# A fixed third expert, and routing tables in other buffers, in a two-layer diffusion backbone with a mixture of experts

## The chip, the cores and the metric

The kernel runs on one core of a Trainium2 chip. The metric is the device time of one execution in microseconds; the number given for a kernel is the median of its runs. Lower is better.

## The reference, cut to what matters

Two layers work on 512 tokens of width 1024 (and 256 context tokens in the first), all in float32. Each layer has a mixer (layer 0: attention beside a convolution; layer 1: a short gated convolution) and then a mixture of 16 experts, of which every token uses two:

```python
def moe_ffn(h, router_w, router_bias, w_gate, w_up, w_down):
    e_idx, e_w = route(h, router_w, router_bias)      # top 2 of 16 experts for each of 512 tokens
    ...                                               # rows sorted by expert, padded to whole blocks
    def expert_block(args):
        tok, e = args
        xb = jnp.take(h, tok, axis=0, mode="fill", fill_value=0)
        return (jax.nn.silu(xb @ w_gate[e]) * (xb @ w_up[e])) @ w_down[e]
    ...
    y = out[dest].reshape(n_tok, TOP_K, -1) * e_w[..., None]
    return y.sum(axis=1)
```

`w_gate[e]` and `w_up[e]` are 1024 x 512, `w_down[e]` is 512 x 1024: three pieces of 2 MB for each expert. Which expert a token uses is known only when the layer's mixer and its norm are done. The order in which the experts are worked through is free.

## The kernel before, in words

**Blocks.** The kernel pads each expert's rows to blocks of 64 (the reference has 256). Experts with no token get one block, so that every expert is loaded and passed once. Experts are worked through in an order of 16 *positions*. Positions 0 and 1 are always experts 0 and 1. The other fourteen are ranked by their number of blocks and taken alternately from the two ends of the ranking: the smallest, the largest, the second smallest, and so on (constants `rank_tie` and `rank_at`, lines 93 to 97; the ranking itself on VectorE in `route`, lines 1078 to 1119).

**Weight buffers.** There are three sets of three 2 MB buffers, and position p uses set p modulo 3. Two sets are slots of `ring`. The third, used by positions 2, 5, 8, 11 and 14, is `mid` (gate weights), `hT_cat` (up weights) and `big` (down weights). These three buffers have other uses before: `hT_cat` holds the transposed tokens until the router's product ("route", l, 0), `big` holds the normalised tokens until they have been stored to `xhat_d` in DRAM, and `mid` holds tables of the routing.

**The loading queue.** SyncE issues all weight loads, in program order, from `load_experts` (line 481). For each layer: positions 0 and 1 as soon as the ring slots come free during the mixer and the first products of the routing; then a wait for `route_ready` (all tables made) and for two gathers of tokens (`hg_in` at 32), a read of the third expert's number from `order_i`, and the three loads of position 2 (lines 498 to 504). From position 3 on, `load_next` waits for each piece until the same piece of three positions ago has been used (`used[k]`: gate, up and down products counted), and `two_before` lets no more than two loads be in flight.

**Routing.** TensorE makes the router's logits, VectorE goes through about a hundred small dependent steps (line 1018 on), TensorE counts and spreads the tables, and the last step signals `route_ready`. The tables are seven: `oh_slot`, `in_blk`, `oh_blk`, `val_blk`, `ranks_above`, `oh_order`, `order_tmp`. All seven are views of `mid`. Smaller vectors are views of `apad` (`rtmp`).

**The expert loop.** GpSimd gathers 64 rows of a block (as 128 half rows, 256 KB) from `xhat_d` by an indirect DMA into `kv_buf` (line 1277), ScalarE copies them on (line 751), TensorE transposes them (line 1589), VectorE and ScalarE scale them into `hgT` (lines 1139 and 742), and TensorE makes the gate product (line 1604), the transposes of the block before (line 1611), the up product (1604 again) and the down product of the block before (line 1620). So an expert's down product comes one block after its gate and up products. VectorE scales the result and GpSimd scatters it to `y_d` (line 1287). `kv_buf` and `prob` hold the keys, values and probabilities of the attention in layer 0 and are idle during routing, except that half of `prob` holds the router's rows until line 1562 has read them.

Of the kernel before, what the change touches and what calls it, by code (L numbers as in the profile page):

```python
# [26 lines left out]
P = 128  # L27
# [6 lines left out]
KT = TT + CT  # L34
# [5 lines left out]
APAD = SEQ + 2 * PAD  # L40
SC_K = 3
NE, NG, EPG = 16, 4, 4
BLK = 64
MAXB = SEQ * 2 // BLK + NE
NB = MAXB + 3
# [19 lines left out]
def build_consts():  # L65

    p = np.arange(P)
    parts = []

    def add(name, a):  # L70
        a = np.asarray(a, np.float32).reshape(P, -1)
        at = sum(x.shape[1] for x in parts)
        CONSTS[name] = (at, at + a.shape[1])
        parts.append(a)

    add("ident", np.eye(P))
    add("ones", np.ones((P, P)))
    add("before", p[:, None] < p[None, :])

    add("sel_both", np.stack([p % 32 == 0, p % 32 == 1], 1))  # L80
    add("sel_x", np.repeat((p % 32 == 0)[:, None], P, 1))
    add("sel_expert", p[:, None] % 32 == np.arange(NE)[None, :])
    add("slot_of_col", np.tile(p % BLK, (P, 1)))

    add("half", p // BLK)
    add("out_offset", p // BLK + 2 * NIDX)
    add("full_blocks", np.tile(np.arange(SEQ // BLK) * BLK - (np.arange(SEQ // BLK) == 0), (P, 1)))
    add("block_slots", np.tile(np.arange(NB + 1) * BLK, (P, 1)))
    add("group_key", np.tile(NG - np.arange(NG), (P, 1)))
    add("expert_key", np.tile(NE - np.arange(NE), (P, 1)))  # L90


    rank_at = [0, 1] + [r for k in range((NE - 2) // 2) for r in (NE - 1 - k, 2 + k)]
    add("rank_at", np.tile(rank_at, (P, 1)))
    tie = NE - 1 - np.arange(NE)
    tie[0:2] = NE * (MAXB + 1) * np.array([3, 2])
    add("rank_tie", np.tile(tie, (P, 1)))
    add("expert_id", np.tile(np.arange(NE), (P, 1)))
    add("expert_before", np.tile((np.arange(NE)[None, :] < np.arange(NE + 1)[:, None]).ravel(), (P, 1)))
    token = np.arange(TT)[None, :, None] * P + p[:, None, None] + np.zeros((1, 1, 2))  # L100
    token = token.transpose(0, 2, 1)
    add("token_row", 2 * token)
    add("out_row", 2 * (token + SEQ * np.arange(2)[None, :, None] - NIDX))
    add("minus_half", np.full((P, 1), -0.5))
    t = np.arange(SEQ)
    inv = (np.float32(10000.0) ** (-np.arange(HD // 4, dtype=np.float32) / np.float32(HD // 4))).astype(np.float32)
    ang = np.concatenate([(t // GRID_W).astype(np.float32)[:, None] * inv,
                          (t % GRID_W).astype(np.float32)[:, None] * inv], -1).astype(np.float32)
    for name, f in (("cos", np.cos), ("sin", np.sin)):
        add(name, f(ang.astype(np.float64)).reshape(TT, P, HD // 2).transpose(1, 0, 2))  # L110
    return np.ascontiguousarray(np.concatenate(parts, 1))
# [62 lines left out]
GROUP_AT = {name: n for n, name in enumerate(GROUPS)}  # L174
# [3 lines left out]
def hybrid_backbone_kernel(nc, x, c, ctx, c_ctx, w_mod, b_mod, norm_mix_g, norm_ffn_g, ev_w_in,  # L178
# [4 lines left out]
    with stack:  # L183
# [11 lines left out]
        mid = sb("mid", [P, 4096])  # L195
# [88 lines left out]
        start_cmp = rtmp(NE + 1, NE)  # L284
        start_f = rtmp(NE + 1)
        place2, blk2, slot2, w2 = (rtmp(2, TT) for _ in range(4))
        assert rt_at[0] <= 4 * APAD

        mid_at = [0]

        def mtmp(**shape):

            n = int(np.prod(list(shape.values())))
            a = mid[:, mid_at[0]:mid_at[0] + n]
            mid_at[0] += n
            return a.rearrange(f"p ({' '.join(shape)}) -> p {' '.join(shape)}", **shape)

        oh_slot = mtmp(n=8, s=P)
        in_blk = mtmp(n=8, b=NB + 1)
        oh_blk = mtmp(n=8, b=NB)  # L300
        val_blk = mtmp(n=8, v=3, b=NB)
        ranks_above = mtmp(e=NE, o=NE)
        oh_order = mtmp(j=NE, e=NE)
        order_tmp = mtmp(j=NE, e=NE)
        assert mid_at[0] <= 4096

        def const(name):
            a, b = CONSTS[name]
# [155 lines left out]
        def _(sp):  # L464
# [16 lines left out]
            def load_experts(l, next_units):  # L481
                def two_before(i, par, k):


                    if k < 2:
                        par, k = par - 1, k + 1
                    else:
                        k = 0
                    slot = EXPERT_SETS[l][par % 3][k]
                    sp.wait_ge(unit_in[slot], i * 16 + (moe_base[l][slot] + (1 if par >= 0 else 0)) * 16)  # L490

                for par in range(2):
                    for k, w in enumerate(("wg", "wu", "wd")):
                        prev = unit_prev[(w, l, par)]
                        sp.wait_ge(acc_done, GROUP_AT[unit_last[prev]] + 1)
                        load_third(l, par, par, k)

                sp.wait_ge(route_ready[l], 1)
                sp.wait_ge(xhat_stored[l], 16 * TT)
                sp.wait_ge(hg_in[l], 32)  # L500
                e = sp.value_load(order_i[0:1, 2:3], min_val=2, max_val=NE - 1)
                for k in range(3):
                    two_before(0, 2, k)
                    load_third(l, e, 2, k)
                used = (gate_done[l], up_done[l], down_done[l])

                def load_next(j, i, par):

                    e = sp.value_load(order_i[0:1, bass.ds(j, 1)], min_val=2, max_val=NE - 1)
                    end = sp.value_load(block_start[0:1, bass.ds(j - 2, 1)], min_val=1, max_val=MAXB)  # L510
                    for k in range(3):
                        two_before(i, par, k)
                        sp.wait_ge(used[k], end)
                        load_third(l, e, par, k)

                with sp.Fori(1, NE // 3) as i:
                    for par in range(3):
                        load_next(i * 3 + par, i, par)
                load_next(NE - 1, NE // 3, 0)
                end = sp.value_load(block_start[0:1, NE - 2:NE - 1], min_val=NE - 2, max_val=MAXB)  # L520
                total = sp.value_load(block_start[0:1, NE:NE + 1], min_val=NE, max_val=MAXB)
                for k, name in enumerate(next_units[0:3]):
                    sp.wait_ge(used[k], end)
                    load_dense(name)
                sp.wait_ge(down_done[l], total)

                sp.wait_ge(y_stored[l], total * 16 + 16)
                for t in range(TT):
                    for k in range(2):
                        rows = y_d[l][(k * SEQ + t * P) * 2:(k * SEQ + (t + 1) * P) * 2, :].rearrange("(p h) n -> p (h n)", h=2)  # L530
                        sp.dma_start(y_in[t][:, k, :], rows).then_inc(yin[l][t], 16)  # L531
                for name in next_units[3:]:
                    load_dense(name)
# [1176 lines left out]
```

## Time and profile before

| | us |
|---|---|
| median of 3 runs | 1397.66 |
| lowest and highest run | 1397.36, 1401.35 |
| span of the profiled execution | 1399.6 |
| TensorE matmul busy | 1237.5 (88%) |
| TensorE weight load busy | 642.5 (46%) |
| VectorE, ScalarE, GpSimd busy | 434.6, 349.9, 334.8 |

The profiled execution has no separate time of its own beside its span of 1399.6 us, which lies 1.9 us over the median of the runs and between their lowest and highest. Matmul busy time is an upper bound of useful work, since matmuls are pipelined and their ends are modelled.

The page also cuts the span into 40 slices of 35 us; each digit is a busy share in tenths (9 is 90% or more), PEclk the granted TensorE clock in tenths of full speed, DMA the share of the 16 DMA engines. The expert stages are slices 14 to 22 and 32 to 39:

```
PE   4899969888898399999999769999985799999992
PEclk9999986887799699999999989999997899999996
DMA  9918771110014299879899680401335798989995
```

### The profile page before, as it was taken

The page shows a single profiled execution, that of the slowest core. Times are in us where ns is not written, and L with a number is a line of the kernel's source. Part 1 is how long each engine was busy: PE and PEld are TensorE (multiplying, and loading weights), DVE is VectorE, ACT ScalarE, POOL GpSimd, SP SyncE. Part 2 cuts the span into 40 slices and gives each one's busy share as a digit, 9 for nine tenths or more (in the row PEclk, how much of TensorE's full clock was granted, in tenths as well). Part 3 has the DMA queues.
Part 4 walks back from the last instruction along what each step waited for, and adds up shares of the span by engine and source line. Part 5 has one row for each costly group of instructions (what it writes and reads, how often), then busy time and mean ns, then how long its engine had stood idle before and what let it go on. Part 6 is the DMA issues. An engine that isn't in the chain of part 4 may idle for free. (4 is left out here: it accounts for less than half of the span.)

```text
span 1399.6 us, 18544 instructions
## 1 busy us (share of the span) xinstructions
PE 1237.5 (88%) x6619; PEld 642.5 (46%) x6620; DVE 434.6 (31%) x951; ACT 349.9 (25%) x670; POOL 334.8 (24%) x491
## 2 busy tenths in 40 slices
PE   4899969888898399999999769999985799999992
PEld 1744425444444255555555334444442455555550
DVE  1222775763223422222222241111226122222223
ACT  2311115564402132222222220000011322222220
POOL 1000059940000123333333220000010333333331
PEclk9999986887799699999999989999997899999996
DMA  9918771110014299879899680401335798989995
GB/s 336 352 61 297 262 282 61 61 61 0 1 60 164 105 392 389 319 289 347 319 394 395 251 333 0 163 18 57 124 105 195 272 388 324 366 324 391 396 367 194
DMA packets 138558, 322.47 MB, mean 230 GB/s; under 512 B 7452, under 2 KB 8520, under 8 KB 138514
## 3 DMA queue, kind: packets, MB, share of 16 engines
q1 hardware_dynamic: 127250, 294.44, 57.1%
q0 software_dynamic: 8640, 23.09, 4.5%
q10 hardware_dynamic: 2624, 4.33, 0.8%
q8 instruction: 30, 0.49, 0.1%
q14 instruction: 14, 0.11, 0.0%
HBM read 307.15 MB, written 19.92 MB: 234 GB/s over the span
## 5 line engine op out<-in xcount | busy, mean ns | idle before, releaser
L1604 PE MATMUL bank<-ring,apad 128*64 128x256 f32 x2176 | 251.7, 385 | 6.3 <-ACT apad L742 3.2
L1604 PEld LDWEIGHTS bank<-ring,apad 128*64 128x64 f32 x2176 | 156.3, 139 | 99.7 <-issue 29.0
L1682 PE MATMUL bank<-hT_cat,ring 128*128 128x512 f32 x384 | 165.0, 592 | 1.0 <-ACT hT_cat L612 1.0
L1620 PE MATMUL scores<-ring,apad 128*64 128x512 f32 x544 | 124.2, 598 | 1.9 <-DVE apad L1156 1.9
L742 ACT ACTIVATE apad<-scores,modcol,mod_a 128x64 f32<-128x64 f32 x208 | 67.2, 403 | 210.3 <-PE scores L1589 210.3
L1682 PEld LDWEIGHTS bank<-hT_cat,ring 128*128 128x128 f32 x384 | 72.9, 190 | 92.5 <-issue 91.4
L1274 POOL COPY cur_idx<-row_i 128x1 int32 (+1 forms) x56 | 10.1, 181 | 383.2 <-ACT apad L751 307.2
L1238 POOL TENSOR_SCALAR stats<-stats 128x1 f32<-128x1 f32 x18 | 8.5, 471 | 343.9 <-ACT mid L602 332.8
L1162 DVE SCALAR_TENSOR_TENSOR prob<-scores,slot_w,qT 128x512 f32<-128x512 f32 x50 | 37.6, 751 | 132.8 <-PE scores L1620 132.8
L925 DVE SCALAR_TENSOR_TENSOR mid<-apad,taps,mid 128x512 f32<-128x512 f32 x90 | 75.6, 880 | 0.6
L1152 DVE TENSOR_TENSOR apad<-apad,bank 128x256 f32<-128x256 f32 x50 | 21.1, 421 | 175.6 <-PE bank L1604 175.6
L1620 PEld LDWEIGHTS scores<-ring,apad 128*64 128x64 f32 x544 | 36.4, 136 | 65.6 <-issue 65.6
L1277 POOL DMA_INDIRECT kv_buf<-xhat_d,cur_idx x56 | 59.5, 1063 | 28.4 <-issue 27.2
L1156 DVE COPY apad<-bank 128x256 f32<-128x256 f32 x50 | 21.2, 425 | 144.8 <-PE bank L1611 144.8
L760 ACT ACTIVATE apad<-bank 128x256 f32<-128x256 f32 x50 | 19.2, 384 | 186.5 <-PE bank L1604 186.5
L760 ACT ACT_TABLE_LOAD x50 | 64.2, 1283 | 0.9
L1470 PE MATMUL scores<-kv_buf,qT 64*128 64x256 f32 (+1 forms) x128 | 63.4, 627 | 0.0
L1139 DVE TENSOR_SCALAR apad<-bank,mod_a,modcol 128x64 f32<-128x64 f32 x208 | 57.2, 338 | 19.1 <-PE scores L1589 14.7
L1282 POOL TENSOR_TENSOR kv_buf<-prob,cst 128x512 f32<-128x512 f32 x52 | 53.7, 1032 | 35.3 <-DVE prob L1162 35.2
L1287 POOL DMA_INDIRECT y_d<-kv_buf,cur_idx x52 | 54.9, 1055 | 28.3 <-issue 28.3
L1604 PE MATMUL bank<-hT_cat,apad 128*64 128x256 f32 x512 | 58.8, 382 | 0.0
L1620 PE MATMUL scores<-big,apad 128*64 128x512 f32 x256 | 58.5, 598 | 0.0
(248 smaller groups left out, 1557.9 us busy)
## 6 DMA issues: line engine op xcount, KB each, us to landing
ring<-in_w_mod SPq DMA_DIRECT2D x24, 2048.0 KB, 17.3
ring<-in_moe_w_gate SPq DMA_DIRECT2D x22, 2048.0 KB, 11.6
ring<-in_moe_w_up SPq DMA_DIRECT2D x22, 2048.0 KB, 11.8
ring<-in_moe_w_down SPq DMA_DIRECT2D x22, 2048.0 KB, 11.2
mid<-in_moe_w_gate SPq DMA_DIRECT2D x10, 2048.0 KB, 11.3
hT_cat<-in_moe_w_up SPq DMA_DIRECT2D x10, 2048.0 KB, 12.0
big<-in_moe_w_down SPq DMA_DIRECT2D x10, 2048.0 KB, 11.4
ring<-in_od_w_in SPq DMA_DIRECT2D x6, 2048.0 KB, 19.2
```

The source lines that it names most:

```text
L742: act.activation(hgT[:, j, :], hg_act_ps[:, at:at + BLK], ACT.Identity, bias=shift_of(l, 3, 0)(j), scale=mod_a[:, 1 + 2 * l, j:j + 1]).the ...
L760: act.activation(silu_g, gate_ps[:, 0:256], ACT.Silu).then_inc(silu_ready[l], 1)
L925: ins = V.scalar_tensor_tensor(out=conv_y[:, i, :], in0=src, scalar=w, in1=conv_y[:, i, :], op0=ALU.mult, op1=ALU.add)
L1139: V.tensor_scalar(hgT[:, j, :], hg_dve_ps[:, at:at + BLK], mod_a[:, 1 + 2 * l, j:j + 1], shift_of(l, 3, 0)(j), ALU.mult, ALU.add).then_inc ...
L1162: V.scalar_tensor_tensor(out=y_blk, in0=y_ps, scalar=slot_w[:, bass.ds(b, 1)], in1=gate_ffn[:, :], op0=ALU.mult, op1=ALU.mult).then_inc(y_ ...
L1277: G.indirect_dma_start(out=hg_raw, out_offset=None, in_=xhat_d, in_offset=bass.IndirectOffsetOnAxis(ap=cur_idx[:, 0, :], axis=0), bounds_c ...
L1282: G.tensor_tensor(y_out, y_blk, const("ones")[:, 0:1].to_broadcast([P, 512]), ALU.mult).then_inc(y_moved[l], 1)
L1287: G.indirect_dma_start(out=y_d[l], out_offset=bass.IndirectOffsetOnAxis(ap=cur_idx[:, 1, :], axis=0), in_=y_out, in_offset=None, bounds_ch ...
L1470: mm = T.matmul(score_ps[n % 2][:, a:b], qT[r, pair, qt * P:(qt + 1) * P], kT2[r, pair // 2, a:b], start=True, stop=True)
L1604: mm = T.matmul(ps[h * BLK:(h + 1) * BLK, 0:256], hgT[:, k, :], w[:, k, h * 256:(h + 1) * 256], start=(k == 0), stop=(k == KD - 1))
L1620: mm = T.matmul(y_ps[h * BLK:(h + 1) * BLK, :], actT[:, k % 2, (k // 2) * BLK:(k // 2 + 1) * BLK], wd[:, k, h * 512:(h + 1) * 512], start= ...
L1682: mm = T.matmul(ps[:, :], w[n][:, k, i * P:(i + 1) * P], hT_cat[:, k, :], start=(k == 0), stop=(k == KD - 1))
```

## The change

Three edits. Position 2 becomes expert 2, always, as positions 0 and 1 already are experts 0 and 1; the other thirteen are ranked and alternated as before, with the middle one of the ranking last. SyncE issues the three loads of position 2 after the router's product and after the stores to `xhat_d`, ahead of the waits for `route_ready` and the two gathers. The tables leave `mid`: `oh_slot` and `val_blk` go to `kv_buf`, four others to `prob`, and `order_tmp` to `apad`.

```diff
-    rank_at = [0, 1] + [r for k in range((NE - 2) // 2) for r in (NE - 1 - k, 2 + k)]
+    rank_at = [0, 1, 2] + [r for k in range((NE - 3) // 2) for r in (NE - 1 - k, 3 + k)] + [3 + (NE - 3) // 2]
     add("rank_at", np.tile(rank_at, (P, 1)))
     tie = NE - 1 - np.arange(NE)
-    tie[0:2] = NE * (MAXB + 1) * np.array([3, 2])
+    tie[0:3] = NE * (MAXB + 1) * np.array([4, 3, 2])
...
-        def mtmp(**shape):
-            n = int(np.prod(list(shape.values())))
-            a = mid[:, mid_at[0]:mid_at[0] + n]
...
+        def ttmp(home, **shape):
+            n, at = int(np.prod(list(shape.values()))), table_at[home]
+            flat = kv_buf[:, :] if home == "kv_buf" else prob[:, :, :].rearrange("p a b -> p (a b)")
...
-        oh_slot = mtmp(n=8, s=P)
-        in_blk = mtmp(n=8, b=NB + 1)
-        oh_blk = mtmp(n=8, b=NB)
-        val_blk = mtmp(n=8, v=3, b=NB)
-        ranks_above = mtmp(e=NE, o=NE)
-        oh_order = mtmp(j=NE, e=NE)
-        order_tmp = mtmp(j=NE, e=NE)
+        oh_slot = ttmp("kv_buf", n=8, s=P)
+        val_blk = ttmp("kv_buf", n=8, v=3, b=NB)
+        in_blk = ttmp("prob", n=8, b=NB + 1)
+        oh_blk = ttmp("prob", n=8, b=NB)
+        ranks_above = ttmp("prob", e=NE, o=NE)
+        oh_order = ttmp("prob", j=NE, e=NE)
+        order_tmp = rtmp(NE, NE)
...
-                sp.wait_ge(route_ready[l], 1)
+                sp.wait_ge(acc_done, GROUP_AT[("route", l, 0)] + 1)
                 sp.wait_ge(xhat_stored[l], 16 * TT)
-                sp.wait_ge(hg_in[l], 32)
-                e = sp.value_load(order_i[0:1, 2:3], min_val=2, max_val=NE - 1)
                 for k in range(3):
                     two_before(0, 2, k)
-                    load_third(l, e, 2, k)
+                    load_third(l, 2, 2, k)
+                sp.wait_ge(route_ready[l], 1)
+                sp.wait_ge(hg_in[l], 32)
                 used = (gate_done[l], up_done[l], down_done[l])
```

## Rows read from the trace of the kernel before

**Rows 1.** Busy time by window, whole core: window, length, busy (instructions), PEclk, DMA share, GB/s.
```profile
460.00:480.00 20.00, 3.71 (x16) 3.49 (x16) 10.77 (x30) 0.00 (x0) 3.35 (x7) 0.59 0.12 45
...
740.00:760.00 20.00, 20.00 (x154) 10.81 (x150) 4.65 (x13) 5.48 (x13) 6.08 (x11) 1.00 1.04 395
...
1340.00:1360.00 20.00, 20.00 (x148) 10.50 (x146) 4.97 (x13) 6.57 (x13) 6.25 (x11) 1.00 1.04 397
```

**Rows 2.** Waits of TensorE, 490 to 800 us: us in total, times, longest.
```profile
PE bank L1604 <- ACT apad L742: 1.6, 1, 1.6
...
PE scores L1620 <- DVE apad L1156: 1.0, 1, 1.0
```

**Rows 3.** Timeline of TensorE, first blocks of layer 0: start, length, instruction.
```profile
503.12 3.65 PE L1620 MATMUL scores<-ring,apad 128*64 128x512 f32 x16
506.60 3.62 PE L1604 MATMUL bank<-mid,apad 128*64 128x256 f32 x32
...
518.20 3.62 PE L1604 MATMUL bank<-ring,apad 128*64 128x256 f32 x32
```

**Rows 4.** Timeline of SyncE's queue, both layers: start, length of the issue, load.
```profile
448.63 0.37 SPq L479 DMA_DIRECT2D ring<-in_moe_w_up  x1
453.35 0.37 SPq L479 DMA_DIRECT2D ring<-in_moe_w_down  x1
486.51 0.40 SPq L479 DMA_DIRECT2D mid<-in_moe_w_gate  x1
...
520.12 0.37 SPq L479 DMA_DIRECT2D ring<-in_moe_w_gate  x1
...
537.64 0.37 SPq L479 DMA_DIRECT2D mid<-in_moe_w_gate  x1
...
1062.01 0.37 SPq L479 DMA_DIRECT2D ring<-in_moe_w_down  x1
1094.57 0.38 SPq L479 DMA_DIRECT2D mid<-in_moe_w_gate  x1
```

**Rows 5.** Busy time in windows of 3 us (columns as in group 1).
```profile
459.00:462.00 3.00, 0.00 (x0) 0.00 (x0) 2.69 (x13) 0.00 (x0) 0.00 (x0) 0.69 0.85 347
...
477.00:480.00 3.00, 0.00 (x0) 0.00 (x0) 0.00 (x0) 0.00 (x0) 2.31 (x5) 0.54 0.28 87
...
1068.00:1071.00 3.00, 0.00 (x0) 0.00 (x0) 2.73 (x11) 0.00 (x0) 0.00 (x0) 0.50 0.82 336
```

**Rows 6.** VectorE's four scalings of a block, before and beside weight loads (timeline).
```profile
481.90 1.10 DVE L1139 TENSOR_SCALAR apad<-bank,mod_a,modcol 128x64 f32<-128x64 f32 x4 [7.56 <-PE scores L1589]
...
493.08 1.10 DVE L1139 TENSOR_SCALAR apad<-bank,mod_a,modcol 128x64 f32<-128x64 f32 x4
```

**Rows 7.** The gathers: timeline of two, their follower, and line 1277's landing times.
```profile
476.34 1.31 POOL L1277 DMA_INDIRECT kv_buf<-xhat_d,cur_idx  x1 [0.65 <-POOL tick L1229]
...
480.01 0.63 ACT L751 ACTIVATE apad<-kv_buf 128x512 f32<-128x512 f32 x1 [23.38 <-DMA kv_buf<-xhat_d,cur_idx]
...
1084.63 1.16 POOL L1277 DMA_INDIRECT kv_buf<-xhat_d,cur_idx  x1 [0.54 <-POOL tick L1229]
...
DMA to landing us min/median/max: 3.4/6.2/7.9
```

**Rows 8.** TensorE in layer 1: gate product of position 12, up product of position 15.
```profile
1322.95 3.62 PE L1604 MATMUL bank<-ring,apad 128*64 128x256 f32 x32
...
1361.67 3.67 PE L1604 MATMUL bank<-ring,apad 128*64 128x256 f32 x32
```

**Rows 9.** SyncE's last loads in layer 1, and landing time of the last up load.
```profile
1334.87 0.37 SPq L479 DMA_DIRECT2D big<-in_moe_w_down  x1
1338.86 0.37 SPq L479 DMA_DIRECT2D ring<-in_moe_w_gate  x1
1344.90 0.37 SPq L479 DMA_DIRECT2D ring<-in_moe_w_up  x1
...
ring<-in_moe_w_up SPq DMA_DIRECT2D x1, 2048.0 KB, 12.1
```

More of the change, by code:

```diff
@@ L286, in hybrid_backbone_kernel @@
         place2, blk2, slot2, w2 = (rtmp(2, TT) for _ in range(4))
-        assert rt_at[0] <= 4 * APAD
-        mid_at = [0]
-        def mtmp(**shape):
-            n = int(np.prod(list(shape.values())))
-            a = mid[:, mid_at[0]:mid_at[0] + n]
-            mid_at[0] += n
-            return a.rearrange(f"p ({' '.join(shape)}) -> p {' '.join(shape)}", **shape)
-        oh_slot = mtmp(n=8, s=P)
-        in_blk = mtmp(n=8, b=NB + 1)
-        oh_blk = mtmp(n=8, b=NB)
-        val_blk = mtmp(n=8, v=3, b=NB)
-        ranks_above = mtmp(e=NE, o=NE)
-        oh_order = mtmp(j=NE, e=NE)
-        order_tmp = mtmp(j=NE, e=NE)
-        assert mid_at[0] <= 4096
+        assert rt_at[0] + NE * NE <= 4 * APAD
+        table_at = {"kv_buf": 0, "prob": 0}
+        def ttmp(home, **shape):
+            n, at = int(np.prod(list(shape.values()))), table_at[home]
+            flat = kv_buf[:, :] if home == "kv_buf" else prob[:, :, :].rearrange("p a b -> p (a b)")
+            table_at[home] += n
+            return flat[:, at:at + n].rearrange(f"p ({' '.join(shape)}) -> p {' '.join(shape)}", **shape)
+        oh_slot = ttmp("kv_buf", n=8, s=P)
[5 more added lines that the diff above has]
+        order_tmp = rtmp(NE, NE)
+        assert table_at["kv_buf"] <= 3 * KT * P and table_at["prob"] <= 2 * KT * P
         def const(name):
```

## The prediction, made blind

> **What bounds the kernel now.** I read the 40 slices first, then the busy time by window over both expert stages, then TensorE's waits there, then the timelines of SyncE's queue and of TensorE side by side. The two expert stages together take 17 of the 40 slices, some 590 us, and in them TensorE is never idle for more than a moment: 20.00 us of every 20 us, at a granted clock of 1.00, in both layers [rows 1]. DMA shows the same fullness there, a share of 1.04 at 395 and 397 GB/s, so the reader has to ask which of the two carries the stage. The waits answer it. Between 490 and 800 us TensorE has five kinds of wait, none longer than 1.6 us in all and none for a weight load; the two that belong to the expert stage, at its start and its end, are 1.6 and 1.0 us [rows 2]. Blocks follow each other every 11.6 us (518.20 - 506.60) [rows 3]. TensorE sets the pace and the loads keep up with it. The stretch in front of the experts is another matter: in 460 to 480 us TensorE is busy for 3.71 us, VectorE for 10.77, DMA for a share of 0.12 [rows 1]. There the end is set by VectorE's chain of small steps, then by the tables, then by the first gather. The weights are not in that chain: the first two experts have landed by then.
>
> **What was to be gained, part by part.** The change fills the quiet DMA in front of the experts. First the size of the move. Position 2's gate load is issued at 486.51 us in layer 0 and at 1094.57 in layer 1 [rows 4]. After the change it waits only for position 1's up load to have landed, since the router's product and the stores are older. That up load was issued at 448.63, with the down load behind it at 453.35, and DMA stays full until about 461.6 (347 GB/s in the window 459 to 462, which is 2.6 us at full rate) [rows 4, 5]. So the new loads stand in the queue from about 457 us and their data follow without a gap: three pieces of 2.1 MB at 395 GB/s, 5.3 us each, 16 us in all. They end at about 477.6. In layer 1 the same sum starts from 1070.5 (336 GB/s in 1068 to 1071) and ends at 1086.5. Position 2 thus arrives about 25 us sooner than now.
>
> What is this worth? TensorE begins with position 2 at 506.60, in the same breath in which the down product before it ends (503.12 + 3.65 = 506.8) [rows 3]. It waits for nothing there. The removed exposure is zero, so 25 us earlier buys 0 us. The same holds for layer 1, where every window of 20 us from 1120 to 1360 is as full as the one shown [rows 1]. The number of blocks stays as it is: TensorE's gate products give 26 in layer 0 and 24 in layer 1, and reordering experts changes neither.
>
> **The tables.** The same VectorE instructions with the same shapes write to other addresses: 0 us. What hid a cost before, if there was one, was the silent DMA; now 395 GB/s go into SBUF beside the chain. The nearest rows are VectorE's four scalings of a block: 1.10 us before any weight load of the stage is issued and 1.10 us with two in flight [rows 6]. I take 0. The removed read of `order_i` on SyncE stood in front of a load that nobody waited for: 0 too. Behind SyncE's new waits stand only position 2's loads and those of position 3, and the latter had the same two conditions before.
>
> **The first gather.** This is the one transfer on the chain that the moved loads can meet. Now it finds DMA empty: issued at 476.34, its data pass in the window 477 to 480 (87 GB/s, 0.26 MB), and ScalarE has it at 480.01, 3.6 us after the issue [rows 5, 7]. Beside two loads a gather takes up to 7.9 us to land, against 3.4 at best [rows 7]. So the bounds are 0 and 4.3 us for each layer. Which end is nearer follows from the times: GpSimd's instruction ends at 477.65 and the loads at 477.6, so layer 0 pays about nothing; in layer 1 it ends at 1085.79 and the loads at 1086.5, an overlap of 0.7 us. With one load's tail in front it can't wait much longer than that tail: 0.1 + 0.7 = 0.8 us for both, bounds 0 and 8.6.
>
> The Trainium skill, page "DMA: Bandwidth & Descriptors", section "Queues, rings and completion order", says that each DMA engine takes turns between its queues, packet by packet, so a gather in GpSimd's own queue should hardly notice SyncE's. By that the term would be 0 and the forecast 0.8 us lower. The trace disagrees in size: landing times of the same gather differ by more than a factor of two [rows 7].
>
> **The later order.** Here the change gives something back. With expert 2 pinned, the alternation has thirteen experts left and ends differently. The blocks of each position can be read from how long TensorE stays on each buffer set. In layer 1 they are 1,1,1,4,1,3,1,2,1,2,1,2,1,1,1,1. How many blocks expert 2 has is not in the trace; the reference's routing on its own inputs gives 25 rows (1 block) in layer 0 and 65 rows (2 blocks) in layer 1, and its totals of 26 and 24 blocks are those of the trace. So layer 0 becomes 1,1,1,1,4,1,3,1,3,1,2,1,2,1,2,1 and layer 1 becomes 1,1,2,1,4,1,3,1,2,1,2,1,1,1,1,1. In layer 1 a two-block expert has moved from near the end to the start, and five single ones close the row instead of four.
>
> A single one costs TensorE 11.6 us but DMA 17.5 (three loads, 520.12 to 537.64) [rows 4]. The reserve shrinks by 5.9 us at each. What starts the final run is the down product of the last two-block expert, whose buffer the down load three positions later needs. Now that is position 11: position 12 starts at 1322.95 [rows 8], the down load follows at 1334.87, 11.9 us later, and then the last gate load at 1338.86 and the last up load at 1344.90. That up load lands 12.1 us on, at 1357.0, and is used at 1361.67: a reserve of 4.7 us [rows 8, 9]. After the change there is one more single expert between the same two points, so the reserve is 4.7 - 5.9 = -1.2 us. The last gate load is issued 6.0 us before the up load and is used some 3.6 us before it (the length of a gate product [rows 3]), so it keeps about 1 us. With the reserve gone TensorE waits about 1.2 us once, in the up product of position 15 of layer 1. Bounds: 0 (a cadence of 16.3 us an expert or less) and 3 (18 us, and a landing half a microsecond later).
>
> Two other places get tighter without breaking. At the start of layer 0, position 3's down load waits for position 0's down product (506.8), so position 4's gate load follows at about 507.3, lands 12 us later at 519.3, and is used at 518.20 + 11.6 = 529.8, with 10 us to spare; its up load has a little less. In layer 0's tail two-block experts stand at positions 12 and 14, more reserve than now.
>
> **The sum.** Against the profiled execution: 1399.6 + 0 (weights) + 0 (tables) + 0.8 (gathers) + 1.2 (tail) = 1401.6. That execution was 1.9 us over the median of the runs, so the forecast for a median is 1399.7.
>
> **The rivals.** A difference of 0.3% is 4.2 us, about what a measurement of this kernel can tell from no change; below, same means within it.
>
> *The loads were the bound after all* (faster). For it: DMA at 1.04 through most of the stage. Against: no wait for weights. If the early load freed everything that TensorE waits for in an expert stage (1.6 and 1.0 us [rows 2]), in both layers, it would give 5.2 us: 1392.5. I give it 0.04.
>
> *Forecast and its near kin* (same): nothing to gain, 0 to 4 us lost to the gather's tail and the last expert. 0.78.
>
> *The gather pays in full* (slower). The moved loads run longer than I reckon, by a slower rate or a late start behind the stores, and the first gather of each layer lands beside them as the later ones do, 4.3 us later; with the tail that is 1397.7 + 8.6 + 1.2 = 1407.5. It decides when the loads run 2 us or more past the gather's issue, 476.34 and 1084.63. For it: in layer 1 they already do, by 1.9. Against: only the last piece is still there. 0.11.
>
> *The last experts starve in layer 1* (slower). If a single expert costs DMA 19 us instead of 17.5, three in a row miss by 1.5 us each on top of 1.2: 1397.7 + 0.8 + 5.7 = 1404.2. For it: DMA is at its full share there [rows 1]. Against: the cadence was read in just such a stretch. 0.06.
>
> *The change doesn't do what it says:* SyncE is held before the third load by the landing of position 1's last load or by the stores, and it starts only after 461 us. Then the end moves by up to 4 us and the case becomes the gather's; without that collision the time is 1399. 0.01 beyond the cases above.
>
> **How the numbers follow.** Faster 0.04 and a little for chance in the measurement, 0.05. Slower: 0.11 + 0.06 and a little for the same reason, 0.18. Same: 0.77. The range takes the forecast with its bounds, -1 to +5 us, and part of the way to the gather's case: 1395.5 to 1404.5.
>
> **What would show it.** Right: position 2's gate load is issued near 457 and 1065 us; DMA full in 462 to 477, where it was silent; `route_ready` and the first gather's issue at the same distance from the router's product as now; the first gather landing in 3.6 to 4.5 us; all blocks 11.6 us apart except the last of layer 1, where a wait of about a microsecond for the up weights appears. Wrong: VectorE's steps in the chain longer than now, the first gather at 6 us or more, any wait for weights elsewhere, or experts that start sooner after the router's product than now, for which I have no mechanism.

## The result and the profile after

| | before | after |
|---|---|---|
| median, us (6 runs each, same chip) | 1397.57 | 1407.32 |
| lowest and highest run | 1397.36, 1401.35 | 1403.95, 1413.23 |
| span of the profiled execution | 1399.6 | 1411.3 |

The changed kernel is slower: the ratio is 1.0071, with an interval of 1.0048 to 1.0093. The forecast was 1399.7 us and "same", with a range of 1395.5 to 1404.5 us, and the measured median lies above it. The two profiled executions were each the slowest of their six. The one after ran for 1413.23 us with a span of 1411.3, and the one before matches the run of 1401.35 with its span of 1399.6, so a run's time is its span plus 1.8 to 1.9 us.

The page after, first TensorE's busy line and its slices, with the clock and DMA, and then the chain that ended last:

```profile
PE 1243.2 (88%) x6619; PEld 644.3 (46%) x6620; DVE 434.9 (31%) x951; ACT 349.1 (25%) x670; POOL 332.7 (24%) x491
PE   4899968988898399999999769999984899999992
PEclk9999986877799699999999989999997899999996
DMA  9918771110014789797899580401339596879995
PE 15%; DMA 6%; issue 1%; DVE 0%; SPq 0%; ACT 0%; POOL 0%; POOLq 0%; DVEq 0%; ACTq 0%
PE bank L1604 9%; PE scores L1620 5%; DMA ring<-in_moe_w_up 3%; DMA big<-in_moe_w_down 2%; DMA mid<-in_moe_w_gate 1%; DMA mid<-y_d 1%; PE bank L1589 1%; PE bank L1611 0%; PE scores L1589 0%; DMA kv_buf<-xhat_d,cur_idx 0%; SPq L531 0%; DMA y_d<-kv_buf,cur_idx 0%; DVE xs L1184 0%; DVE xs L1185 0%; DVE apad L1139 0%
```

The number of instructions is the same. DMA is busy earlier in layer 0 (slice 14 is a 7 where it was a 2). The new thing is in the chain of work that ended last: weight loads stand in it, three in a row close to its end. The loads did move as predicted, as SyncE's timeline after shows for both layers and for the last experts of layer 1:

```profile
457.13 0.37 SPq L479 DMA_DIRECT2D ring<-in_moe_w_down  x1
461.39 0.37 SPq L479 DMA_DIRECT2D mid<-in_moe_w_gate  x1
466.66 0.37 SPq L479 DMA_DIRECT2D hT_cat<-in_moe_w_up  x1
472.29 0.37 SPq L479 DMA_DIRECT2D big<-in_moe_w_down  x1
...
1073.38 0.37 SPq L479 DMA_DIRECT2D mid<-in_moe_w_gate  x1
...
1330.79 0.37 SPq L479 DMA_DIRECT2D ring<-in_moe_w_down  x1
...
1347.14 0.37 SPq L479 DMA_DIRECT2D big<-in_moe_w_down  x1
1353.34 0.37 SPq L479 DMA_DIRECT2D ring<-in_moe_w_gate  x1
1358.66 0.37 SPq L479 DMA_DIRECT2D ring<-in_moe_w_up  x1
```

Position 2's gate load is issued 12.7 us after the router's product (448.72), where before it came 41.6 us after it (444.94) [rows 4]. DMA is full where it was nearly silent, while VectorE's chain runs. The windows (columns as in [rows 1]):

```profile
463.00:483.00 20.00, 3.71 (x16) 3.49 (x16) 11.44 (x36) 0.00 (x0) 3.05 (x6) 0.61 0.98 371
477.00:480.00 3.00, 0.57 (x3) 0.32 (x2) 0.52 (x3) 0.00 (x0) 0.38 (x2) 0.89 1.03 410
480.00:483.00 3.00, 0.00 (x0) 0.00 (x0) 0.00 (x0) 0.00 (x0) 2.67 (x4) 0.68 0.70 261
744.00:764.00 20.00, 20.00 (x158) 11.13 (x155) 3.90 (x10) 4.25 (x9) 7.29 (x12) 1.00 1.04 397
1359.00:1371.00 12.00, 10.23 (x76) 5.19 (x72) 2.69 (x7) 3.48 (x7) 3.83 (x7) 1.00 1.05 392
1371.00:1374.00 3.00, 2.86 (x18) 1.74 (x20) 0.00 (x0) 0.00 (x0) 0.00 (x0) 0.66 1.03 412
1374.00:1377.00 3.00, 3.00 (x22) 1.69 (x18) 0.38 (x1) 0.00 (x0) 0.00 (x0) 0.77 0.34 137
```

The third window (480 to 483) holds the first gather of layer 0, with the last moved load still beside it. The middle of the stage is as full as before [rows 1]. At the end, TensorE has lost 1.8 us in 1359 to 1371, and behind that its clock is at 0.66 and 0.77. TensorE's timeline shows what it did there, and at the start of layer 0:

```profile
510.70 3.62 PE L1604 MATMUL bank<-mid,apad 128*64 128x256 f32 x32
...
522.29 3.62 PE L1604 MATMUL bank<-ring,apad 128*64 128x256 f32 x32
...
535.85 3.67 PE L1604 MATMUL bank<-ring,apad 128*64 128x256 f32 x32 [1.79 <-issue]
...
1365.24 3.62 PE L1604 MATMUL bank<-ring,apad 128*64 128x256 f32 x32
1371.14 5.36 PE L1604 MATMUL bank<-ring,apad 128*64 128x256 f32 x32 [1.91 <-DMA ring<-in_moe_w_up]
```

The last line is the up product of position 15. It is the one that was started at 1361.67 before without a wait and took 3.67 us [rows 8]. Now it waits 1.91 us for its weights, and then takes 5.36. The third line, at 535.85, is the gate product of position 4 in layer 0. It waits 1.79 us, and the profile names nothing that released it ("issue"); below I call this a wait without a releaser.

To see what such things sum to, I cut each profiled execution at the starts of fixed instructions: on TensorE the router's product, the first gate product and the last down product of each layer, and on SyncE the first store of the output, where the last row ends. The last row also holds the stretches between the others, the mixer of layer 1 above all:

| stretch, us | before | after | e1 | e5 | e11 |
|---|---|---|---|---|---|
| start to router's product, layer 0 | 444.9 | 448.7 | 445.9 | 448.8 | 440.7 |
| router's product to first gate product, layer 0 | 38.36 | 38.61 | 38.37 | 38.81 | 38.76 |
| experts, layer 0 | 303.16 | 305.24 | 303.38 | 304.78 | 304.74 |
| router's product to first gate product, layer 1 | 37.84 | 38.68 | 38.15 | 38.24 | 37.90 |
| experts, layer 1 | 279.41 | 282.79 | 282.90 | 282.96 | 281.38 |
| all behind the first router's product | 942.8 | 949.9 | 946.5 | 949.5 | 947.7 |

"e1", "e5" and "e11" are repeats of the changed kernel, told below. The first row lies wholly ahead of the first instruction that the change touches. So 3.8 us of the 11.7 between the two spans are not the change's. 7.1 us lie between the router's product and the first store of the output, and 0.8 us behind that.

### The profile page after: what moved, and what is told of

It reads as the page before. It is cut to its first block and busy times, and to the rows that moved or that the text cites. A ratio compares the mean times of both kernels' runs of the same rounds, so it can differ in the third digit from the quotient of the medians.

```text
span 1411.3 us, 18532 instructions
## 1 busy us (share of the span) xinstructions
PE 1243.2 (88%) x6619; PEld 644.3 (46%) x6620; DVE 434.9 (31%) x951; ACT 349.1 (25%) x670; POOL 332.7 (24%) x491
## 5 line engine op out<-in xcount | busy, mean ns | idle before, releaser
L1604 PE MATMUL bank<-ring,apad 128*64 128x256 f32 x2240 | 260.4, 386 | 10.1 <-ACT apad L742 3.1
L1604 PEld LDWEIGHTS bank<-ring,apad 128*64 128x64 f32 x2240 | 161.3, 139 | 107.5 <-issue 32.7
L1682 PE MATMUL bank<-hT_cat,ring 128*128 128x512 f32 x384 | 165.0, 592 | 0.9 <-ACT hT_cat L612 0.9
L1620 PE MATMUL scores<-ring,apad 128*64 128x512 f32 x560 | 127.9, 599 | 1.9 <-DVE apad L1156 1.9
L1365 PE MATMUL bank<-ring,cact 128*32 128x512 f32 x384 | 54.4, 690 | 3.0 <-DMA ring<-in_w_mod 1.7
L1415 PE MATMUL bank<-hT_cat,ring 128*128 128x512 f32 x128 | 57.0, 598 | 0.0
```

Source lines behind the costliest of these rows:

```text
L1365: mm = T.matmul(ps[32 * q:32 * q + 32, :], cact[:, k, :], w[:, k, :], start=(k < 4), stop=(k >= 4))
L1415: mm = T.matmul(ps[:, :], w[:, k, i * P:(i + 1) * P], hT_cat[:, k, :], start=(k == 0), stop=(k == KD - 1))
L1604: mm = T.matmul(ps[h * BLK:(h + 1) * BLK, 0:256], hgT[:, k, :], w[:, k, h * 256:(h + 1) * 256], start=(k == 0), stop=(k == KD - 1))
L1620: mm = T.matmul(y_ps[h * BLK:(h + 1) * BLK, :], actT[:, k % 2, (k // 2) * BLK:(k // 2 + 1) * BLK], wd[:, k, h * 512:(h + 1) * 512], start= ...
L1682: mm = T.matmul(ps[:, :], w[n][:, k, i * P:(i + 1) * P], hT_cat[:, k, :], start=(k == 0), stop=(k == KD - 1))
```

## The experiments

The diffs are against the changed kernel, except for e3. Ratios are to the kernel before, run beside each on the same chip.

**The changed kernel again (e1, e5, e11).** No edit.

> The changed kernel once more, to see which of its losses come back. In its first profile the end lay 11.7 us later: 3.8 us before the router's product of layer 0 (code that is the same in both), 1.1 us at the two first gathers, 1.9 us of waiting for the last up load of layer 1 and 1.7 us of lower clock behind it, 2.2 us of two short TensorE waits without a releaser in layer 0. Theory A (the order starves the last expert, the gather pays a tail): the wait for the last up load and the gathers' 1.1 us come back, 4.7 us in all, the rest is scatter, and the time is 1401.5 to 1403. Theory B (something of the change acts in code that is the same): the 3.8 us before the router come back too, and the time is 1405 to 1410.

> The changed kernel a third time, for the size of the whole difference. Both repeats so far showed the wait of 1.9 us for the last up load of layer 1 and 1.7 us of lower clock behind it. Theory A (order and gathers): 3.6 us and 0.3 to 1.1 us, so 3.9 to 4.7 us over the kernel before, a ratio of 1.003; the 9.9 us of the first measurement were this and a chance difference of the attention stage. Rival B (something of the early load acts in the attention stage): 8 to 10 us again, and start to router's product 3 us longer than in kernels without the early load (it was 448.7 and 445.9 and 445.8 with it, 444.9, 443.1 and 441.1 without).

> The changed kernel as it is, on the same chip. A and B: a wait without a releaser of 0.3 to 1.9 us at position 4's gate product in layer 0, the wait of 1.9 us for the last up load of layer 1, 282.8 to 283.0 us for layer 1's experts.

Measured: e1 has a ratio of 1.0022 (1.0004 to 1.0041), e5 1.0039 (1.0020 to 1.0058), and e11, one execution, took 1402.61 us where the kernel before had a median of 1400.05. (One execution of e1 took 2585.74 us and one of the kernel before beside it 3239.6; both are left out of the ratios, and nothing in the record explains them.) The kernel is slower, by about 5 us, and the 9.8 us of the first comparison were partly chance. Behind the router's product the four profiled executions lose 7.1, 3.7, 6.8 and 4.9 us, 5.6 in the mean. e1's first theory, 4.7 us, is near the mean and lacks the waits of layer 0. Its second, that the 3.8 us ahead of the router's product come back, does not hold: against 444.9, that product starts at 445.9, 448.8 and 440.7. The lines that differ, in order e1, e5, e11 (TensorE's timelines):

```profile
530.91 3.67 PE L1604 MATMUL bank<-ring,apad 128*64 128x256 f32 x32 [0.32 <-issue]
...
1364.89 5.36 PE L1604 MATMUL bank<-ring,apad 128*64 128x256 f32 x32 [1.87 <-DMA ring<-in_moe_w_up]
```
```profile
535.68 3.67 PE L1604 MATMUL bank<-ring,apad 128*64 128x256 f32 x32 [1.90 <-issue]
...
1370.97 5.36 PE L1604 MATMUL bank<-ring,apad 128*64 128x256 f32 x32 [1.88 <-DMA ring<-in_moe_w_up]
```
```profile
527.52 3.67 PE L1604 MATMUL bank<-ring,apad 128*64 128x256 f32 x32 [1.85 <-issue]
...
1362.71 3.67 PE L1604 MATMUL bank<-ring,apad 128*64 128x256 f32 x32 [1.84 <-DMA ring<-in_moe_w_up]
```

The wait for the last up load is there each time, 1.8 to 1.9 us. The slow product behind it is there in three of four. Where it is absent the stage is 1.5 us shorter (281.38). The wait without a releaser varies from 0.3 to 1.9.

**The order alone (e2).** The ranking of the change, with tables and loads as before.

```diff
-                sp.wait_ge(acc_done, GROUP_AT[("route", l, 0)] + 1)
+                sp.wait_ge(route_ready[l], 1)
                 sp.wait_ge(xhat_stored[l], 16 * TT)
+                sp.wait_ge(hg_in[l], 32)
...
+        oh_slot = mtmp(n=8, s=P)      # all seven tables in mid again
```

> The kernel before with the new order of experts alone: expert 2 third, its loads where they were, behind the tables and two gathers; tables in mid. Theory A: the last up load of layer 1 is late here as well, by 1 to 4 us, and the time is 1399 to 1402. Rival (the early load costs, not the order): no wait for weights at the end, 1397.5.

Measured: ratio 1.0071 (1.0050 to 1.0093), the slowest of this group. The stretches behind the router's product lose 7.0 us: 4.1 in the experts of layer 0 (307.23) and 3.6 in layer 1 (282.99), less 0.7 elsewhere. TensorE's timeline and the clock in layer 0:

```profile
529.82 5.36 PE L1604 MATMUL bank<-ring,apad 128*64 128x256 f32 x32 [1.97 <-DMA ring<-in_moe_w_gate]
535.88 3.67 PE L1604 MATMUL bank<-ring,apad 128*64 128x256 f32 x32 [0.33 <-DMA ring<-in_moe_w_up]
...
1365.31 5.36 PE L1604 MATMUL bank<-ring,apad 128*64 128x256 f32 x32 [1.86 <-DMA ring<-in_moe_w_up]
```
```profile
528.00:531.00 3.00, 1.18 (x7) 0.68 (x9) 0.75 (x1) 0.00 (x0) 1.73 (x5) 0.84 1.05 384
531.00:534.00 3.00, 3.00 (x20) 1.78 (x18) 0.00 (x0) 0.00 (x0) 0.99 (x1) 0.59 1.05 390
```

The tail's loss belongs to the order alone. And the order makes a second hole that the whole change doesn't have: four single-block experts now stand in front of the first large one in layer 0, and at the old load time position 4's weights come 2 us late. So the early load does buy something in this stage, 2.0 to 3.9 us (303.38 to 305.24 against 307.23), but only against a hole that its own order has made. Against the kernel before, that is nothing.

**The tables alone (e3).** The kernel before, with the tables in `kv_buf`, `prob` and `apad`.

```diff
-        oh_slot = mtmp(n=8, s=P)
+        oh_slot = ttmp("kv_buf", n=8, s=P)      # and the other six as in the change
```

> The kernel before with the tables moved to kv_buf, prob and apad, and nothing else. All theories: 1397.5, within 1 us. If the tables' new place costs something (VectorE or TensorE slower on them), up to 1 us a layer, 1399.5.

Measured: ratio 1.0003 (0.9983 to 1.0024), and 942.9 against 942.8 us behind the router's product. The move of the tables costs nothing.

**Another order of the ranks (e4).** The whole change, but the ranks from position 3 on are arranged so that a two-block expert is back near the end of layer 1.

```diff
-    rank_at = [0, 1, 2] + [r for k in range((NE - 3) // 2) for r in (NE - 1 - k, 3 + k)] + [3 + (NE - 3) // 2]
+    rank_at = [0, 1, 2, 15, 3, 14, 13, 4, 12, 11, 5, 10, 9, 6, 8, 7]
```

> The changed kernel with another alternation: after the three fixed experts the ranking is read 15, 3, 14, 13, 4, 12, 11, 5, 10, 9, 6, 8, 7, so that in layer 1 a two-block expert stands at position 13 instead of 10. By the cadences (17.5 us of DMA against 11.6 us of TensorE for a single block) the last up load of layer 1 then has about 5 us in reserve. Theory A: no wait there, 3.6 us won on the changed kernel of the same call. Rival (the loss lies elsewhere): the wait goes, the time stays within 1 us of the changed kernel.

Measured: the experts of layer 1 take 279.38 us, as before the change, and TensorE waits for no weights there. That gives the 3.5 us back in its stage. The ratio hardly shows it (1.0020, 1.0005 to 1.0035): in the profiled execution the stretch from layer 0's last down product to layer 1's router's product, the mixer of layer 1, whose code is the same, took 269.3 us where the kernel before took 267.1, and an interval of this width holds 2 us on either side. The stage settles the cause, the median can't.

**That order with the late load (e6).** The order of e4, tables and loads as before.

```diff
+    rank_at = [0, 1, 2, 15, 3, 14, 13, 4, 12, 11, 5, 10, 9, 6, 8, 7]
...
+                sp.wait_ge(route_ready[l], 1)      # loads of position 2 behind the tables and gathers
```

> The kernel before with expert 2 third and the mended alternation (15, 3, 14, 13, 4, ...), loads of position 2 at their old place, tables in mid. Theory A: layer 0 starves at position 4 as in the kernel with the new order alone (2.0 us of waiting for its gate load, 1.7 us of lower clock, 0.3 us for its up load: 4.0 us), layer 1 doesn't: the last up load has 5 us or more in reserve. Time 4 us over the kernel before. Rival (the wait in layer 0 was chance): no wait, time of the kernel before.

Measured: ratio 1.0034 (1.0018 to 1.0050); layer 1's experts 279.56, layer 0's 308.76. The hole of e2 is there again, with two waits in TensorE's timeline:

```profile
533.32 3.67 PE L1604 MATMUL bank<-ring,apad 128*64 128x256 f32 x32 [1.90 <-DMA ring<-in_moe_w_gate]
539.36 5.36 PE L1604 MATMUL bank<-ring,apad 128*64 128x256 f32 x32 [1.99 <-DMA ring<-in_moe_w_up]
```

Against e4 that is 5.1 us in layer 0 for the load time alone (the tables, which differ too, cost nothing by e3).

**Two of the three loads early (e7).** The order of e4; position 2's gate and up loads early, its down load behind the first gathers, so that DMA is quiet when they land.

```diff
-                for k in range(3):
+                for k in range(2):
                     two_before(0, 2, k)
                     load_third(l, 2, 2, k)
                 sp.wait_ge(route_ready[l], 1)
                 sp.wait_ge(hg_in[l], 32)
+                two_before(0, 2, 2)
+                load_third(l, 2, 2, 2)
```

> The changed kernel with the mended alternation, and of position 2 only the gate and up loads early; the down load waits for the tables and two gathers. Theory (the gather pays for the tail of the loads in front of it): the early loads end 5 us sooner, the first gather lands in 3.5 us in both layers, and from router's product to first gate product are 38.4 us in layer 0 and 37.8 us in layer 1 (the kernel before had 38.36 and 37.84, the one with the mended alternation 38.60 and 38.42). No wait for weights. Time 1397 to 1400, that of the kernel before. Rival (busy DMA during the routing is what costs): 0.5 us stay in each layer.

Measured: ratio 1.0015 (1.0001 to 1.0030), the lowest of the versions with the early load and whole loads, though the intervals of e1 and e4 overlap with it. Router's product to first gate product is 38.51 and 37.82 us; the gather reaches ScalarE 3.80 and 3.50 us after its issue, where before it was 3.67 and 3.52. In layer 1 the gather's term is gone. In layer 0 waits without a releaser, 2.9 us in two, took what was won (305.93), so the time of the kernel before, which was expected, was not reached.

**The largest experts first (e8).** With everything else as changed, the ranks go from largest to smallest, so that the reserve is used up as early as it can be.

```diff
+    rank_at = [0, 1, 2] + list(range(3, NE))
```

> The changed kernel with the thirteen free experts from largest to smallest, so that seven (layer 0) and eight (layer 1) single blocks stand last. A single block costs DMA 17.5 us and TensorE 11.6, so once the reserve is gone every further one waits 5.9 us. By a sum of cadences the waits for weights are 11 us in layer 0 and 23 us in layer 1. Theory A with the clock: each wait is followed by a stretch at half the clock, which is hidden where DMA is the bound anyway (the slower product eats the next wait): 34 to 45 us over the kernel before. Rival (TensorE's clock adds a price to each wait also here, 1.7 us apiece): 50 us or more.

Measured: ratio 1.0287 (1.0268 to 1.0306), about 40 us. The experts take 12.4 us more in layer 0 and 22.6 in layer 1. Layer 1's last single experts, TensorE's timeline:

```profile
1338.95 5.36 PE L1604 MATMUL bank<-ring,apad 128*64 128x256 f32 x32 [3.44 <-DMA ring<-in_moe_w_gate]
...
1356.16 5.36 PE L1604 MATMUL bank<-ring,apad 128*64 128x256 f32 x32 [2.70 <-DMA ring<-in_moe_w_gate]
1362.56 3.67 PE L1604 MATMUL bank<-ring,apad 128*64 128x256 f32 x32 [0.67 <-DMA ring<-in_moe_w_up]
...
1373.12 5.36 PE L1604 MATMUL bank<-mid,apad 128*64 128x256 f32 x32 [2.72 <-DMA mid<-in_moe_w_gate]
```

Once the reserve is gone a single expert takes 17.2 and 17.0 us, the time of its three loads, against 11.6 of TensorE's. That is close to the 17.5 from which the prediction took its 5.9 us an expert (here 5.5). A slow product (5.36 us) costs nothing extra in such a run: it falls into time in which the next load isn't there yet, so only 0.6 to 1.0 us of waiting is left for the up load. In the two stages the waits for weights add up to 22.6 us and the slow products to 11 more, 34 of the 35.0 lost.

**Half loads from position 3 on (e9, e10).** The changed kernel, where every load from position 3 on moves half of its piece. The other half of each buffer keeps old data, so the values that come out are not those of the reference; the instructions of TensorE stay the same. It shows what loads cost, and is no candidate.

```diff
+                n = (4 if k == 2 else 8) // share        # share is 2 from position 3 on, else 1
+                sp.dma_start(dst[:, 0:n], src[:, 0:n]).then_inc(unit_in[slot], 16)
```

> The changed kernel, in which every load from position 3 on moves only the first half of its piece (1 MB); the products use old data in the other half, so the values differ, and the work of TensorE stays the same. The loads of positions 0 to 2 and their early start are unchanged. From position 3 on DMA is half idle. Theory A, the wait without a releaser at position 4's gate product in layer 0 (1.8 us in the changed kernel, 1.9 and 0.3 in its repeats) comes from DMA that is full around it, for example the 16 KB instruction packets that pass at 524, 531 and 537 us: it falls to 0.3 us or less, layer 0's experts take 303.2 us (303.16 before). Theory B, it comes from the early start or the order itself and not from full DMA: 0.3 to 1.9 us stays, 304 to 305.2. By both the wait for the last up load of layer 1 goes with its slow product behind it, and that stage takes 279.4 us (282.8 to 283.0 in the changed kernel). Total against before: A -1 to +2 us (ratio 0.999 to 1.001), B 0 to +3. If the ratio is at 1.003 or more, neither the holes nor the wait carry the 5.7 us.

> The same kernel a second time, for a second look, since the wait without a releaser differed between repeats. A: 0.3 us or less again. B: a value between 0.3 and 1.9, and not 0.3 twice, or twice as in the changed kernel's repeats.

Measured: ratio 0.9998 (0.9972 to 1.0024) for e9; e10, one execution, took 1397.64 us. The experts take 302.91 and 302.85 us in layer 0 and 279.29 and 279.10 in layer 1, and behind the router's product it is 942.9 and 943.1 us, against 942.8 before. First e9's windows, then TensorE's waits in layer 0 and in layer 1 that belong to the experts (the kernel's lines are shifted by 2):

```profile
520.00:540.00 20.00, 20.00 (x148) 10.44 (x146) 4.65 (x13) 6.34 (x14) 5.48 (x12) 1.00 0.94 341
1360.00:1366.00 6.00, 6.00 (x52) 3.59 (x50) 1.01 (x3) 0.55 (x2) 1.29 (x3) 1.00 0.07 27
```
```profile
PE bank L1606 <- ACT apad L744: 1.6, 1, 1.6
PE scores L1622 <- DVE apad L1158: 1.0, 1, 1.0
...
PE bank L1606 <- ACT apad L744: 1.6, 1, 1.6
PE bank L1606 <- DVE apad L1141: 1.4, 1, 1.4
```

No wait for a weight is left, and none without a releaser, in both executions. Theory A holds as far as two executions can tell: the waits without a releaser come with full-size loads. The six executions with an early load and full-size loads, e8 aside, all have one at position 4's gate product (the first execution of the changed kernel, e1, e4, e5, e7 and e11), though e1's 0.32 us is no longer than the 0.27 that the kernel before has elsewhere. Even at a DMA share of 0.94 they are gone. And the whole loss of the change goes with the size of the loads: the gathers' term is still there (0.4 and 1.0 us from router's product to first gate product, both layers together), and the expert stages are 0.4 and 0.6 us shorter than before. What the early start and the order cost where loads are never late is zero within the measurement, and what they gain is zero too.

The trace's record of DMA packets says more about this wait. Queue q8 moves instructions, in packets of 16 KB. One of them passes shortly before position 4's gate product (starts in us; "due" is the end of TensorE's work before it):

| | after | e1 | e4 | e5 | e7 | e11 | e9 | e10 |
|---|---|---|---|---|---|---|---|---|
| packet starts | 531.75 | 526.82 | 527.27 | 531.56 | 529.24 | 523.41 | 523.01 | 519.21 |
| product due | 534.06 | 530.59 | 530.67 | 533.78 | 531.46 | 525.67 | 529.24 | 525.55 |
| product starts | 535.85 | 530.91 | 531.37 | 535.68 | 533.34 | 527.52 | 529.24 | 525.55 |
| packet to product | 4.10 | 4.09 | 4.10 | 4.12 | 4.10 | 4.11 | 6.23 | 6.34 |

In all six executions with the wait, it ends 4.1 us after the packet starts, whether it was 0.3 us long or 1.9. In the two without it, the packet is there 6.2 us and more before the product. So TensorE waits here for something that comes a fixed time after this packet, and late code is the plain reading of that.

## Why the prediction was wrong

Most of its mechanism held, and its "same" did not. The four profiled executions give these terms, in us, as means against before:

| term | predicted | measured |
|---|---|---|
| early weights | 0 | 0 (e9) |
| tables | 0 | 0 (e3) |
| first gathers | 0.8 | 0.7 (0.3 and 0.4) |
| last expert of layer 1 | 1.2 (0 to 3) | 3.1 (2.0 to 3.6) |
| experts of layer 0 | 0 | 1.4 (0.2 to 2.1) |
| other stretches behind the router | 0 | 0.5 |
| sum | 2.0 | 5.6 |

The prediction added its 2.0 to a median of 1397.7. With 5.6 in its place the time would be 1403.3: slower by the prediction's own measure of 0.3%, yet still inside its range. What took the first comparison to 1407.32 beyond that, 4 us, did not come back in e1, e5 and e11. I put it down to chance; where such chance lies is told below.

**The step that failed is the tail of layer 1.** Its place was right to the instruction: position 15, the up product, one wait. So was its cause, since it comes with the order alone (e2) and goes with another order (e4, e6). Two things were mis-sized. The first is the wait, 1.9 and not 1.2. The run of loads starts, as reckoned, with the down load that the last two-block expert releases, now position 13's at 1330.79. From there to the last up load it is 27.9 us (1358.66 - 1330.79), where it was 10.0 [rows 9]: 17.8 us for one more single expert, and 17.3 to 17.6 in e1, e5 and e11. In the mean that is the 17.5 of the prediction. What was short is the landing: the product starts 12.5 to 13.0 us after the up load's issue, and the prediction took 12.1. The second, larger one is that the step stopped at the wait. Behind it the next product runs at a lowered clock, 5.36 us in place of 3.67, which is 1.7 more, in three of the four executions. The price is 1.9 + 1.7 = 3.6, over the upper bound of 3 that I gave. The prediction had no term for the clock.

**Layer 0 was given nothing.** Its blocks are 11.6 us apart as predicted, and position 4's weights came in time, though with 7 us to spare and not 10: its gate load was issued at 513.44, had landed by 526.64 at the latest, when the load two places behind it was issued, and was due at 534.06. What came was the wait without a releaser at position 4's gate product, 0.3 to 1.9 us, and one more of 0.4 in the first execution. The kernel before has one of 0.3 at most in all of layer 0. By e9 and e10 it comes with the size of the loads, and it ends a fixed 4.1 us after an instruction packet. That this packet holds TensorE's code is not recorded, and why it is late is not shown: no run moved the packet by itself, and DMA is as full in e1 (share 1.03, wait 0.32) as in e11 (1.04, wait 1.85). With the late load the wait isn't seen, but there TensorE waits 1.97 us (e2) and 1.90 (e6) for weights at the same product, and by the 4.1 us, as an estimate, the packet would have asked for only 0.3 and 0.4. In the kernel before, e3 and e8 position 3 has the largest expert, so that TensorE reaches position 4 several blocks later.

**The rest is chance in code that did not change.** The attention stage (from TensorE's first product of line 1470 to its first of line 1528 behind it) takes 163.2 us in the profile before, 169.4 in the one after. e1 has 166.2, e5 169.4, e11 163.0; e6, with the late load, has 166.5, and e8, with the early one, 163.0. TensorE's granted clock goes with it. In the two windows shown it is 0.74 and 0.74 in the profile before (163.2 us), 0.74 and 0.66 in e1, e4, e6 and e7 (166.2 to 166.5), and 0.66 twice in the one after and in e5 (169.4). The windows before, then after, with the same busy time of TensorE to 0.01 us:

```profile
300.00:320.00 20.00, 18.44 (x74) 10.11 (x72) 10.97 (x21) 11.34 (x22) 0.00 (x0) 0.74 0.00 0
320.00:340.00 20.00, 18.44 (x64) 9.57 (x64) 4.34 (x12) 10.63 (x21) 0.00 (x0) 0.74 0.00 1
```
```profile
300.00:320.00 20.00, 18.45 (x67) 10.20 (x66) 10.35 (x21) 10.88 (x21) 0.00 (x0) 0.66 0.00 0
320.00:340.00 20.00, 18.45 (x64) 9.85 (x63) 4.83 (x12) 10.68 (x21) 0.00 (x0) 0.66 0.00 1
```

The router's product of layer 0 starts at 440.3 to 448.8 us in the profiles with the early load, and at 441.1 to 446.6 in those without, so no effect of the change shows there. The kernel before varies from 1393.7 to 1407.0 us over the later runs, on three chips; steps of 3 us like these would make up a good part of that, though only one of its executions was profiled. I had taken the spread of three runs, 4 us, as all that chance can do. I also read the profiled execution as 1.9 us over the median; it was 3.7, and its span 1.8 below its own time. The two slips cancel in the forecast.

**The rivals.** The loads as the bound: against, since e9 takes half of them away and gains nothing. The gather in full: its 1407.5 is next to the measured 1407.32, but by luck, since its condition was wrong: the gather reached ScalarE after 3.93 and 4.36 us, and not 8. Issue and copy in layer 1, after:

```profile
1091.58 1.16 POOL L1277 DMA_INDIRECT kv_buf<-xhat_d,cur_idx  x1 [0.55 <-POOL tick L1229]
...
1095.94 0.63 ACT L751 ACTIVATE apad<-kv_buf 128x512 f32<-128x512 f32 x1 [23.70 <-DMA kv_buf<-xhat_d,cur_idx]
```

The last experts starving more: its 1404.2 is near the 1403.3 that the change alone would give, but its condition was wrong too. A single expert costs DMA 17.0 to 17.8 us and not 19, and only one of them missed.

VectorE beside full DMA, which the prediction took as 0: right. The longest step of its chain in the routing, and the first gather behind the chain, in the kernel before [rows 7 for its gather] and after:

```profile
467.63 1.23 DVE L1112 TENSOR_TENSOR mid<-apad,cst 128x1024 f32<-128x1024 f32 x1
```
```profile
471.41 1.23 DVE L1112 TENSOR_TENSOR kv_buf<-apad,cst 128x1024 f32<-128x1024 f32 x1
...
480.12 1.31 POOL L1277 DMA_INDIRECT kv_buf<-xhat_d,cur_idx  x1 [0.65 <-POOL tick L1229]
```

The step takes 1.23 us in both and starts 22.69 us after the router's product in both, and the gather is issued 31.40 us after it in both (476.34 - 444.94, 480.12 - 448.72), while DMA's share in 462 to 477 us was 1.03 after.

The rule of turns between queues that the prediction weighed (the Trainium skill, page "DMA: Bandwidth & Descriptors", section "Queues, rings and completion order") would have made the gathers' term 0. The trace agrees in part: with the last moved load still beside it in layer 0, at 261 GB/s in 480 to 483 us, the gather came 0.26 us later than in an idle DMA, and over the four executions the two gathers together cost 0.7 us, near my 0.8.

No version beats the kernel before. Where TensorE fills the stage and waits for no weights, there is nothing that an early load could remove.

## What to carry over

If no product waits for a weight in the profile, an earlier load is worth nothing, and whatever is changed to make it possible is the real edit: here it was the order of the experts. Where two engines run with a reserve, work out the reserve at every place that the new order tightens, with its error, and price a miss as the wait and the slower work behind it. And take the size of chance from the same stretch in several executions, and not from three totals.

## What the runs showed of the hardware

- Behind a wait of TensorE of 1.8 to 2.0 us for weights, the next product (32 matmuls, 128x256) took 5.36 us in place of 3.67 in six cases of eight (one each in the changed kernel's four executions, two in e2, two in e6). The granted clock was 0.66 and 0.77 in the windows behind the one in the changed kernel, and 0.84 and 0.59 in the two windows of the first in e2 (means between the levels of 1.2 GHz, 0.5, and 2.4 GHz, 1.0); it was 1.00 in the window before, in which TensorE was busy but for the wait. Behind four waits of the same length without a releaser it never did; 3.67 us each time. What tells the two apart is open.
- Waits without a releaser, 0.3 to 1.9 us, at a fixed place of the expert loop, beside a DMA share of 1.04 (e11, 520 to 540 us); none at 0.94 and 0.83 (e9, e10). Each ended 4.1 us after a 16 KB instruction packet had started (six executions, 4.09 to 4.12). Where nothing waited, 6.2 and 6.3 us lay between the two.
- One stage of unchanged code takes 163, 166 or 169 us, and the granted clock in it goes along (0.74 and 0.74, 0.74 and 0.66, 0.66 and 0.66 in the same two windows).
- An indirect gather of 256 KB came up to 0.8 us later behind the early loads of 2 MB in another queue than in an idle DMA (3.7 and 3.5 us before; 3.7 to 4.1 in layer 0 and 3.6 to 4.4 in layer 1 over four executions). In the expert stage of the kernel before, beside full DMA, such gathers land in 6.2 us in the median and up to 7.9 [rows 7].
